# GLA decays: one fp32r product over stacked high and low halves, weights split in the gate rows' stage

## The reference, cut to what matters

```
lr = lr_g.astype(f32).reshape(bn, t, 2, GLA_RANK)                      # GLA_RANK = 16
log_a = log_sigmoid(einsum('btdr,dre->dbte', lr, gla_w2) + gla_b2) / GLA_TAU
# per direction, head and chunk; b is the running sum of log_a in the chunk:
S_new = exp(b_end) * S + (k * exp(b_end - b))^T v
o     = (q k^T * exp(b_t - b_s), causal) v + (q * exp(b)) S
```

## Time and profile before

| what | value |
|---|---|
| median of 3 runs | 2597.2 us (2596.54 to 2603.38) |
| profiled execution | 2592.95 us |
| its span, first to last instruction | 2591.2 us |
| TensorE busy | 2267.9 us (88%) |
| VectorE busy | 1424.7 us (55%) |
| ScalarE busy | 1008.7 us (39%) |
| GpSimd busy | 862.4 us (33%) |
| mean granted TensorE clock | 0.918 of full speed |

### The profile page before, as it was taken

One profiled execution on the slowest core, in us unless ns is written; L12 is line 12 of the kernel. 1 busy time (PEld: TensorE's weight loads), 2 busy tenths in 40 slices (PEclk: granted clock), 3 DMA queues, 4 the chain that ended last, 5 costly groups with the idle time before them and its releaser, 6 DMA issues. The chain is left out here.

```text
span 2591.2 us, 27704 instructions
## 1 busy us (share of the span) xinstructions
PE 2267.9 (88%) x10782; PEld 1843.4 (71%) x10782; DVE 1424.7 (55%) x1757; ACT 1008.7 (39%) x1263; POOL 862.4 (33%) x629
## 2 busy tenths in 40 slices
PE   6989979993899997699999959999948999999992
PEld 1278868882788886488888847778746778887882
DVE  1536542103223321588888834543347899999993
ACT  1322211111133333345444433542224666666662
POOL 5300001000235554266666631120012344444441
PEclk9989989995799998599999979999958999999996
DMA  7633243113344554433345357564237985549525
GB/s 280 220 73 98 74 171 118 49 49 111 125 147 138 142 155 117 152 98 114 110 119 134 102 161 224 169 197 142 86 153 271 367 292 148 163 147 329 174 57 162
DMA packets 254845, 397.68 MB, mean 153 GB/s; under 512 B 26934, under 2 KB 176566, under 8 KB 247932
## 3 DMA queue, kind: packets, MB, share of 16 engines
q1 hardware_dynamic: 224876, 242.26, 29.9%
q0 software_dynamic: 28112, 148.41, 18.1%
q10 hardware_dynamic: 1728, 5.25, 0.6%
HBM read 401.55 MB, written 88.67 MB: 189 GB/s over the span
## 5 line engine op out<-in xcount | busy, mean ns | idle before, releaser
L2581 DVE TENSOR_TENSOR ex_w_lo<-ex_raw,ex_w_hi 128x2048 fp32r<-128x2048 f32 x186 | 416.4, 2285 | 41.0 <-ACT ex_w_hi L2555 40.4
L2555 ACT ACTIVATE ex_w_hi<-ex_raw 128x2048 fp32r<-128x2048 f32 x182 | 337.6, 1910 | 180.4 <-DMA ex_raw<-in_w_up_dram,w_rows 93.5
L670 POOL DMA_DIRECT2D vals<-rows_stage x40 | 21.9, 548 | 438.5 <-ACT rows_stage L662 438.5
L2457 POOL DMA_INDIRECT ex_raw<-in_w_up_dram,w_rows x60 | 82.4, 1373 | 133.2 <-DVE ex_w_lo L2581 121.3
L1996 DVE TENSOR_TENSOR mo_w_lo<-mo_w,mo_w_hi 128x1024 fp32r<-128x1024 f32 x48 | 59.7, 1244 | 102.2 <-ACT mo_w_hi L1893 102.0
L882 PE MATMUL gl_u_ps<-half_hi,gl_u_w_hi 128*128 128x512 f32 x256 | 111.8, 437 | 3.5 <-ACT gl_u_exp L900 3.5
L1531 PEld LDWEIGHTS gl_lv_ps<-gl_q_level,gl_k_level 128*128 128x128 f32 x896 | 108.6, 194 | 8.5 <-issue 3.4
L2457 POOL DMA_INDIRECT ex_raw<-in_w_down_dram,w_rows x30 | 50.6, 1688 | 184.9 <-DVE ex_w_lo L2581 178.6
L1531 PE MATMUL gl_lv_ps<-gl_q_level,gl_k_level 128*128 128x64 f32 x896 | 110.7, 276 | 1.3 <-DVE gl_scores L1661 0.7
L882 PE MATMUL ml_u_ps<-half_hi,ml_u_w_hi 128*128 128x512 f32 x256 | 104.1, 407 | 8.0 <-ACT ml_u_exp L900 8.0
L2107 PE MATMUL mo_ps<-mo_branch_hi,mo_w_hi 128*128 128x512 f32 x256 | 105.6, 412 | 5.9 <-DVE mo_w_lo L1996 5.5
(11 more groups left out here) (402 smaller groups left out, 6311.4 us busy)
## 6 DMA issues: line engine op xcount, KB each, us to landing
fr_w<-in_w_mod_dram SPq DMA_DIRECT2D x12, 2048.0 KB, 9.8
ml_u_w<-in_w_in_dram SPq DMA_DIRECT2D x32, 512.0 KB, 5.2
gl_u_w<-in_w_in_dram SPq DMA_DIRECT2D x32, 512.0 KB, 5.1
vals<-rows_stage POOLq DMA_DIRECT2D x40, 256.0 KB, 2.3
ml_v<-vals SPq DMA_DIRECT2D x20, 512.0 KB, 3.9
gl_v<-vals SPq DMA_DIRECT2D x20, 512.0 KB, 3.4
qk_w<-in_w_in_dram SPq DMA_DIRECT2D x16, 512.0 KB, 4.7
rows_w<-in_w_in_dram SPq DMA_DIRECT2D x8, 1024.0 KB, 6.4
```

The source lines that it names most:

```text
L2457: pool.indirect_dma_start(out=raw[:, q, :], out_offset=None, in_=sources[q], in_offset=bass.IndirectOffsetOnAxis(ap=m.w_rows[:, q, b:b + 1 ...
L2555: act.activation(hi[:, q, h], raw[:, q, h], ACT.Copy).then_inc(hi_done[q], 1)
L2581: dve.tensor_tensor(lo[:, q, at], raw[:, q, at], hi[:, q, at].bitcast(F32), ALU.subtract)\
```

## The change

`m.lr` now has 96 partitions and type fp32r: the rounded (high) rows of the tokens at partitions 0 to 31 and again at 32 to 63, the low rows at 64 to 95. VectorE makes high and low of the 64 PSUM rows at once, and SyncE places them with six DMAs from SBUF to SBUF. The weights lie likewise in a new tile `m.rank_w`: high at 16 to 31, low at 48 to 63, high at 80 to 95. One product over 96 rows so gives high x high + low weights x high tokens + high weights x low tokens. The weights are loaded and split in `gate_rows`; `gla_scan` loses its own tile, its clearing, its two loads and TensorE's wait for them.

```diff
@@ project_qk @@
+        lr_hi = sb("qk_lr_hi", [64, T], F32R)
+        lr_lo = sb("qk_lr_lo", [64, T], F32R)
@@ SyncE, loop over tiles @@
                     load(s + 2)
+                if s == 2:
+                    sp.wait_ge(small_left, 4)
+                    for at, src in ((0, lr_hi), (32, lr_hi), (64, lr_lo)):
+                        for d in range(2):
+                            sp.dma_start(m.lr[at:at + 32, d, :].bitcast(F32), src[32 * d:32 * d + 32, :].bitcast(F32))\
+                                .then_inc(lr_placed, 16)
...
+            sp.wait_ge(lr_placed, 16 * 6)
@@ VectorE, s == 1 @@
-                    for d in range(2):
-                        dve.tensor_copy(m.lr[:, d, :], ps[0][32 * d:32 * d + 32, 0:T]).then_inc(small_left, 1)
+                    dve.tensor_copy(lr_hi[:, :], ps[0][0:64, 0:T]).then_inc(small_left, 1)
+                    dve.wait_ge(small_left, 3)
+                    dve.tensor_tensor(lr_lo[:, :], ps[0][0:64, 0:T], lr_hi[:, :].bitcast(F32), ALU.subtract)\
+                        .then_inc(small_left, 1)
@@ gate_rows, SyncE after the fetches of km and qm @@
+        rank_raw = sb("gr_rank_w", [96, 2, HEADS * DK])
+            sp.wait_ge(rank_cleared, 1)
+            for at in (16, 48, 80):
+                sp.dma_start(rank_raw[at:at + RANK, :, :], w["gla_w2"][0].rearrange("d r n -> r d n"))\
+                    .then_inc(rank_loaded, 16)
             sp.wait_ge(step, 18)
@@ GpSimd @@
+            pool.memset(rank_raw[:, :, :], 0.0).then_inc(rank_cleared, 1)
@@ VectorE, after L782 @@
+            dve.wait_ge(rank_loaded, 16 * 3)
+            dve.tensor_copy(m.rank_w[:, :, :], rank_raw[:, :, :]).then_inc(rank_split, 1)
+            dve.wait_ge(rank_split, 1)
+            dve.tensor_tensor(m.rank_w[32:64, :, :], rank_raw[32:64, :, :], m.rank_w[32:64, :, :].bitcast(F32),
+                              ALU.subtract).then_inc(rank_split, 1)
             dve.wait_ge(turned, 1)
@@ gla_scan @@
-        w2 = sb("gl_w2", [32, 2, H * DK])
-            sp.wait_ge(w2_cleared, 1)
-            for d in range(2):
-                sp.dma_start(w2[16:32, d, :], w["gla_w2"][0, d]).then_inc(w2_loaded, 16)
-            pool.memset(w2[:, :, :], 0.0).then_inc(w2_cleared, 1)
-                if u == 0:
-                    pe.wait_ge(w2_loaded, 32)
-                else:
+                if u:
                     pe.wait_ge(ket_ready, min(u, STEPS - 2))
                     pe.wait_ge(z_ready, u)
-                    last = pe.matmul(z_ps[:, h * P:(h + 1) * P], w2[:, d, h * DK:(h + 1) * DK],
+                    last = pe.matmul(z_ps[:, h * P:(h + 1) * P], m.rank_w[:, d, h * DK:(h + 1) * DK],
@@ build @@
-            m.lr = place(gla, "lr", [32, 2, T])
+            m.lr = place(gla, "lr", [96, 2, T], F32R)
+                m.rank_w = place(gla, "rank_w", [96, 2, HEADS * DK], F32R, side="right")
```

More of the change, by code:

```diff
@@ L393, in project_qk @@
         bias = sb("small_bias", [GATE_ROWS, 2])
+        lr_hi = sb("qk_lr_hi", [64, T], F32R)
+        lr_lo = sb("qk_lr_lo", [64, T], F32R)
+        lr_placed = sem("qk_lr_placed")
         ps = [ctx.enter_context(nc.psum_tensor(f"qk_ps{j}", [P, 3 * 512], F32)) for j in range(2)]
@@ L697, in gate_rows @@
         step, actd, turned, moved = (sem(f"gr_{n}") for n in ("step", "act_step", "turned", "moved"))
+        rank_raw = sb("gr_rank_w", [96, 2, HEADS * DK])
+        rank_cleared, rank_loaded, rank_split = (sem(f"gr_{n}") for n in ("rank_cleared", "rank_loaded", "rank_split"))
         fetched, rows_stored = sem("gr_fetched"), sem("gr_rows_stored")
@@ L718, in _ @@
             sp.wait_ge(rows_stored, 64)
+        @block.gpsimd
+        def _(pool):
+            pool.memset(rank_raw[:, :, :], 0.0).then_inc(rank_cleared, 1)
         @block.scalar
@@ L1270, in gla_scan @@
         q_exp = sem("gl_q_exp")
-        half_loaded, w2_cleared, w2_loaded = sem("gl_half_loaded"), sem("gl_w2_cleared"), sem("gl_w2_loaded")
+        half_loaded = sem("gl_half_loaded")
         (cleared, z_made, z_ready, z_abs, log_ready, la_ready, b_ready, ex_in, ex_ready, lv_in, lv_exp, qk_ready,
```

## The result

The changed kernel takes 2573.1 us (median of 4 runs, 2570.9 to 2573.8), the kernel before 2596.9 beside it; the ratio is 0.9905, interval 0.9883 to 0.9927. The forecast was 2584, range 2576 to 2598. The direction and the cheaper pass came true; the clock, which the forecast put at nothing, did not stay as it was. The gain is 24 us where 13 were forecast, and the time lies 3 us under the range. A second set of five runs of the changed kernel gave 2571.4 beside 2592.3, ratio 0.9915 (0.9897 to 0.9934).

What follows compares the result with a forecast made beforehand. The GLA scan was taken as a latency chain first, then bound by TensorE. Decay passes at full clock 7.0, at half clock 4.3, and the start 1.8 made 13.1 us off the 2597.2 median: 2584, range 2576 to 2598.

Steps and rivals of the forecast that it cites:

- the cheaper pass: Decay matmuls (L1501): four passes a call, not eight, saving 0.50 us at full clock (7.0) and 0.85 at half (4.3).
- the clock term: GLA output steps: as many drops to 1.2 GHz as before, six of 13 steps at 0.94, so zero.
- a thinner stretch as what could bring falls: Second rival, chance 0.07: thinner short matmuls bring 22 more drops to 1.2 GHz, 30.6 us, giving 2615.
- The fall's price: GLA steps: each stretch at 1.2 GHz costs 1.39 us, a step taking 27.15 in place of 25.76.
- the 27.72: One GLA step at full clock takes 27.72 us because a store of the gates lands late.
- the third rival: GLA steps: the next resource, VectorE busy 79%, takes over the 7.0 us, leaving 6.1: 2591; chance 0.13.
- First rival: Decay matmuls: fp32r below 256 columns costs its cycles four times over; gain 3.9 us, 2593; chance 0.22.
- The start: GLA start without the weight clearing, loads and wait: 1.8 us saved, bounds 0 and 4.0.
- The chain: GLA start: ScalarE's gate-unit weight halves (L865) wait for DMA, then comes copy L1450, which the second decay call awaits.
- SyncE's earlier queue: GLA start: first k load goes out at 1025.8 in place of 1027.65, 1.85 us earlier.
- The zeros: Added work in the gate rows' and projection stages costs 0; at most 1.8 us without cover and 2.4.
- The low end of the range: Upper bounds of the passes, 5.9 us more, and two drops of the clock fewer: 2576.

Runs made afterwards that it cites:

- before_96_rows: Kernel before with its fp32 decay matmuls over 96 rows in place of 32, the 64 added rows zeros: 2585.9 us, ratio 0.9974.
- before_again: The kernel before, unchanged, run once more for a second profile: 2591.4 us, ratio 0.9998.
- early_weights: Kernel before with only its old fp32 weight tile cleared and loaded in the gate rows' stage: 2589.5 us, ratio 0.9985.
- two_pass_32: Changed kernel with decay matmuls in plain fp32 (two passes) over the first 32 rows only: 2590.5 us, ratio to before 0.9993.
- one_pass_32: Changed kernel with its fp32r decay matmuls over the first 32 rows only: 2572.7 us, ratio to before 0.9924.
- two_pass: Changed kernel with decay matmuls reading the same stacked tiles as plain fp32, two passes over 96 rows: 2584.9 us, ratio to before 0.9966.
- double_calls: Changed kernel with each decay call's four fp32r matmuls issued twice into the same places: 2582.7 us, ratio to before 0.9959.
- level1_first: Changed kernel with level 1 ahead of the decay call in the output steps: 2585.1 us, ratio to before 0.9961.
- start_wait: Changed kernel with the old clearing, two loads and TensorE's wait put back at the GLA start on an unread tile: 2574.5 us, ratio to before 0.9922.
- gate_before_decays: Changed kernel with the first two of eight gate-unit slices moved between level 0 and the decay call: 2601.7 us, ratio to before 1.0032.
- store_first: Changed kernel with SyncE's store of gate unit 2n-2 ahead of the load of unit 2n+3: 2577.9 us, ratio to before 0.9944.

## Why the prediction was off in size

**The step that failed** is the clock term: "With as many falls as today this term is zero, which I take". Today's six falls behind the decay call went to none, in all six profiles of kernels with this product. The 13 steps lost 12.3 us. before_96_rows, with the old two passes and no falls, stands between (344.4, 338.2, 332.1): 6.2 us for what went with the falls, 6.1 for shorter passes (13 x 0.47). The sign was wrong as well: I named a thinner stretch as what could bring falls, and counted its shorter length only as a reason against that. A second sentence failed with it: "The contraction of 96 rows in place of 32 changes no term". The pass does last the same (calls of 1.15 and 1.16 us), but before_96_rows, which changes nothing else, is 6.4 us faster, because its falls are gone.

What the runs show: with two passes over 32 rows there are 4 to 6 falls behind the decay call in each of four profiles (before, before_again, early_weights, two_pass_32), 20 in all, each beginning 2.2 to 2.5 us after the call. Without the second pass (one_pass_32), with 96 rows (before_96_rows, two_pass, double_calls) and with both changes there is none at that place. The change removed both, either would have done. Whether the rows themselves count or the 0.19 us by which they shorten the thin stretch is not shown; no run has one without the other.

**The fall's price** was right outside the silu steps (27.15 against 25.76) and too high inside them, where an undisturbed step takes 26.85 and a fall adds 0.3. I had read the 27.72 as one stray late store; a late store was the rule in four steps, at 26.85, and this one step took 0.9 more. With the falls gone the store shows in all four. So the six falls were worth 5.2 us and not 8.3 (three outside the silu steps 4.3, three inside 0.9), and the long step 0.9. Early_weights has such a step too (28.09); why is open.

**The pass.** Forecast 0.50 us a call at full clock and 0.85 at half; the call got 0.49 shorter (0.66) and 0.96 (1.11). A pass is issued every (1.11 - 0.475)/3 = 0.21 us at half clock, as forecast; my 0.85 took four spacings, but the last pass ends 0.1 sooner too, since an fp32r pass lasts 475 ns there in place of 578. At full clock the gate unit follows the decay call after 2.25 us (1241.25 to 1243.50 above) in place of 2.89 (1147.15 to 1150.04), 0.64 less; yet the step lost only 0.47. The rest, 0.17, comes back ahead of levels 4 to 6, where TensorE's loads now wait 8.0 us, 13 times, in place of 3.2, 7 times. In before_96_rows it is the same: the stretch is 0.19 us shorter and the step still takes 25.76. That is the third rival in small: VectorE's copies are about to take over, and level1_first shows it. First rival: wrong, 128 columns in fp32r pass at 0.12 to 0.13 us. The Trainium skill's 81 ns for such a pair (page "TensorE: Matmul & The Clock Gate", "Back-to-back issue gap") is not reached here either: (0.66 - 0.274)/3 = 0.129 us.

**The start.** 2.4 us in place of 1.8, in one pair of profiles; the medians of early_weights and start_wait do not size it. The chain was the one named: ScalarE's second L865 now starts at 1038.24, 11.2 us after the stage start in place of 13.6, and the copy comes behind it. SyncE's earlier queue gives 1.85; the rest is that the weights, issued at 1028.84, landed a little faster. GpSimd's clearing had indeed become a limit on VectorE's side (1.30 us of wait), hidden behind ScalarE.

**The zeros held.** The gate rows' stage starts and ends 0.34 us later, as long as before; the added work stands in VectorE's gap, 7.94 us of which are left:

```profile
629.24 0.68 DVE L805 CAST rank_w<-gr_rank_w 96x1024 fp32r<-96x1024 f32 x1
629.95 1.22 DVE L807 TENSOR_TENSOR rank_w<-gr_rank_w,rank_w 32x1024 fp32r<-32x1024 f32 x1
...
639.10 0.53 DVE L810 COPY g_col<-gr_cols 128x360 f32<-128x360 f32 x1 [7.94 <-PE gr_decps L825]
```

In the projection stage the cast and the subtraction take 1.48 us each, and the six placing DMAs hold SyncE from 166.3 to 170.5, before the next load is due at 173.2.

**From the profile to the median.** I carried a gain from one profile of the kernel before (2592.95) to a median 4.25 us above it. Executions of that kernel spread from 2585 to 2603 in all sets, those of the changed one from 2568 to 2574; the falls that move between executions are a likely part of that spread. The counts of falls are known for two of them only, but slower executions do have the lower mean clock: the correlation is -0.73, -0.30 and -0.62 over the 17, 23 and 26 executions of the three sets. Outside GLA the first pair of profiles differs by 2.8 us against the changed kernel and the second by 2.8 in its favour. Of the first, 0.3 stand ahead of the mLSTM stage, where the edits are, and the rest where no edit is; I take it for the scatter of one execution each. The low end of the range adds up to 2575.4 and not 2576; the result lies under both.

**Left open.** The falls of level1_first, gate_before_decays and store_first come with 96 rows and one pass, so these two are no guard against falls in levels 4 to 6. Each of those falls stands behind a wait for VectorE's level copies; but the fourth silu step of the changed kernel has such a wait (1.14 us) and no fall, so the wait alone does not decide. What does is not settled.

## What to carry to other kernels

When a small product with few contraction rows sits in a stretch of short matmuls, look at the granted clock of every step, not of the stage: the number of steps at 0.94 is a term of the sum, with its own price, and a change there moves it. Look also where in the step the stretch at 1.2 GHz begins: the same 0.94 came from two places here. Filling the contraction, even with zeros, and cutting passes both kept the clock up behind the decay call, while reordering for a covered wait of 0.32 us cost 12 to 29 us. Before putting a wait down as stray, compare the same step of the loop in a second profile: a slower neighbour may hide it in the first.

## What the runs showed of the hardware that was not expected

A plain fp32 matmul over 96 rows, 64 of them zero in both operands, let the clock stay at 2.4 GHz where the same over 32 rows let it drop to 1.2 GHz in 4 to 6 of 13 steps; one such stretch, in the kernel before:

```profile
1224.43:1226.90 2.47, 2.47 (x20) 1.00 0.97 295
1226.90:1230.30 3.40, 3.40 (x12) 0.50 0.21 63
1230.30:1251.58 21.28, 20.96 (x119) 1.00 0.35 106
```

The fall begins within the diagonal. From the decay call to the gate unit TensorE counts as busy all the time in both kernels (2.89 of 2.89 us, 2.70 of 2.70). The Trainium skill says on the page "TensorE: Matmul & The Clock Gate", section "What's actually happening", that the clock follows how busy the engine has been; the rows agree only if "busy" means more than having an instruction in the array. Whether it is the occupied rows that count, or how long the thin stretch lasts, these runs do not separate.

A plain matmul over 32 rows also costs time behind it: the same two groups of short matmuls start 0.08 and 0.18 us later behind a call over 32 rows than behind one over 96, while the calls themselves take 1.15 and 1.16 us.
